# Expert loop of a hybrid decoder block: the narrow down product moves beside the wide one, into a PSUM bank of its own, and the wide gate turn moves ahead of the row turns

## The chip, the cores and the metric

The kernel runs on one NeuronCore of a Trainium2 chip. The metric is the device time in microseconds (us) of one execution. It is the median of three runs, and lower is better. The profile is of one further execution, and its own time stands beside its span in the table below.

## What is computed

One decoder layer on 512 tokens of width 1024 in float32: a mixer (gated linear attention, sparse attention, mLSTM) and then a mixture of 64 experts. The change is in the experts alone:

```python
w = sigmoid scores of the 6 chosen experts, normalised, times 2.5; gates[t, e] = w or 0
a = einsum('td,edf->tef', xb, w_gate);  u = einsum('td,edf->tef', xb, w_up)     # d = 1024, f = 256
routed = einsum('tef,efd->td', silu(a) * u * gates, w_down)
shared = (silu(t @ s_gate) * (t @ s_up)) @ s_down
return routed + shared
```

Only the rows that were routed to an expert are multiplied by its weights, so each chosen (token, expert) pair is one row of work, and the 3 MB of weights of an expert are read once for each unit of rows that uses them.

## The kernel before, in words

**Units and steps.** The routed rows are packed into units. A wide unit has up to 128 rows of one expert, a narrow unit up to 64 rows of one expert. One step of the expert loop works on one wide and one narrow unit. The number of steps is found at run time; here there are 31, of which 30 are iterations of a hardware loop that every engine runs (`with pe.Fori(0, more) as i` and its like on ACT, DVE, POOL and SP), and one stands behind the loop. The loop is software-pipelined: iteration i ends with the wide gate and up product of step i+1.

**Weights.** A step needs six pieces of 1 MB, each with one buffer in `ring`: of the wide expert piece 0 and 1 (gate and up columns, for two halves of d) and piece 2 (down), and the same three of the narrow expert. `load_piece(e, b, k)` issues them on SP's queue (L629 for gate and up, two DMAs each; L633 for down), b = 0 for wide, 1 for narrow. SP issues in program order, and waits ahead of each until the buffer is free: wide 0 and 1 (of step i+1), narrow 2 (of step i, free when `down_used` tells that the last narrow down product is done), wide 2 (of step i+1), narrow 0 and 1 (of step i+1).

**Wide products.** They are exact to nearly float32 by a split: ACT copies a wide piece to a rounded high part (`gate_hi` L1782, `down_hi` L1789), DVE subtracts to get the low part (`weights_lo`, L2477), which also frees the ring buffer. The same is done to the rows (`turned`, L1795 and L2497) and to the gated activations (`act_turned`, L1812 and L2532). PE makes high*high, low*high and high*low products: `gate_up` (L1351 and L1355, 24 matmuls into bank 2) and `down` (L1410, 12 matmuls into banks 4 and 5).

**Narrow products.** They are plain float32, straight from the ring: `gate_up_narrow` (L1368, into bank 3) and `down_narrow` (L1394, which went into bank 4, so that it had to wait until DVE had read the wide result out of that bank, `y_read`).

**Turns.** PE transposes: the gathered rows of the wide unit (`turn`, L1331, banks 0 and 1) and of the narrow unit (`turn_narrow`, L1338, bank 7, read by ACT's L1800), the gated activations of the wide unit (`act_turn`, L1377, bank 6) and of the narrow one (`act_turn_narrow`, L1383, bank 6, read by ACT's L1812).

**Between.** ACT's silu is L1806, DVE's product with it L2504 (`gated`). DVE scales the results out of PSUM into `ys` (`store_y` L2518, `store_narrow` L2526), and POOL scatters them to `y_dram` (L812) and gathers the rows of later units (L785) by indirect DMA. `store_narrow` waits until the narrow scatter of the step before has landed (`y_stored1`).

**Order.** Each engine's order is written out by hand, and engines meet only at semaphores. Behind the loop come `down` and `down_narrow` of the last step (the last narrow one went into bank 7 already), the load of the six result rows of each token, their sum, and the final norm.

Of the kernel before, what the change touches and what calls it, by code (L numbers as in the profile page):

```python
# [145 lines left out]
def hybrid_kernel(nc, a, out):  # L146
# [7 lines left out]
    WIDE, NARROW = 128, 64  # L154
# [8 lines left out]
    with ctx:  # L163
        sems = {}

        def sem(name):
            if name not in sems:
                sems[name] = ctx.enter_context(nc.semaphore(name))
            return sems[name]
# [11 lines left out]
        bank = [ctx.enter_context(nc.psum_tensor(f"bank{i}", [P, 512], F32)) for i in range(BANKS)]  # L181
# [148 lines left out]
        w_raw = [pieces(ringf, w_at[b]) for b in range(2)]  # L330
        w_shd = w_raw[0][0].rearrange("p (m n) -> p m n", m=2)
        diag = w_raw[0][1].rearrange("p (i k t) -> p i k t", i=TT, t=P)
        LAST_NARROW = 7
        SUMMED = (3, 3, 3, 2)
        w_hi, w_lo = pieces(arenap, 0), pieces(arenap, 6144)
        re.at = 12288
# [3 lines left out]
        ys = [rx.take(D) for _ in range(2)]  # L340
# [6 lines left out]
        ae = ro.take(2, NARROW)  # L347
# [496 lines left out]
        def _(pe):  # L844
            mm = nc.tensor.matmul
# [125 lines left out]
            for f in range(2):  # L971
                b = begin(f"kd{f}")
                for i in range(TT):
                    ins = nc.tensor.transpose(b[:, tile_cols(i)], kd[:, f, tile_cols(i)], ident[:, :])
# [10 lines left out]
            for l in range(8):  # L985
# [5 lines left out]
                for tp in range(2):  # L991

                    pair = [begin(f"scA{l}{2 * hh + tp}") for hh in range(2)]
                    for ii in range(2):
                        for f in range(2):
                            t = tile_cols(2 * tp + ii)
                            for hh, b in enumerate(pair):
                                r_ = slice(64 * hh, 64 * hh + 64)
                                ins = mm(b[:, tile_cols(2 * ii + f)], ksrc[r_, f, t], qsrc[r_, f, t], start=True, stop=True)
# [8 lines left out]
            for h in range(5):  # L1008
                if h < 4:
                    b = begin(f"oA{h}")  # L1010
                    for i in range(TT):
                        if i:
                            mm(b[:, tile_cols(i)], state[:, i - 1, h // 2, :], qcz[h % 2][:, h // 2, tile_cols(i)],
                               start=True, stop=False)
                        ins = mm(b[:, tile_cols(i)], va[:, i, tile_cols(h)], S[:, h % 2, i, h // 2, :],
                                 start=(i == 0), stop=True)
# [13 lines left out]
            for i in range(TT):  # L1030
                ins = nc.tensor.transpose(b[:, 4 * i:4 * i + 4], g4[3][:, tile_cols(i)], ident[0:4, 0:4])
# [14 lines left out]
            for h in range(4):  # L1046
# [11 lines left out]
                if h == 3:  # L1058
                    pe.wait_ge(sem("squares_ready"), 9)
                    b = begin("msq")  # L1060
                    for k in range(2):
                        ins = mm(b[:, :], ones[:, :], sqB[:, k, :], start=(k == 0), stop=(k == 1))
# [5 lines left out]
                for j in range(TT):  # L1068
                    pe.wait_ge(sem("SW_ready"), 4 * h + j + 1)
                    ins = mm(b[:, P * j:T], vc[:, j, tile_cols(h)], SW[:, j, P * j:T], start=(j == 0), stop=(j == 3))  # L1070
                end(ins)
                b = begin(f"den{h}")
                for j in range(TT):
                    ins = mm(b[:, P * j:T], ones[:, :], SW[:, j, P * j:T], start=(j == 0), stop=(j == 3))
# [24 lines left out]
            for i in range(TT):  # L1099
                ins = nc.tensor.transpose(b[:, 32 * i:32 * i + 32], small[0:32, tile_cols(i)], ident[0:32, 0:32])  # L1100
# [48 lines left out]
            for n in range(-1, 8):  # L1149
                if n < 7:  # L1150
                    i, g = divmod(n + 1, 2)
# [11 lines left out]
                i, g = divmod(n, 2)  # L1163
# [163 lines left out]
            def turn(half):  # L1327

                rows = xg[0].rearrange("t (p j) -> t j p", j=8)
                for q in range(4):  # L1330
                    ins = nc.tensor.transpose(bank[half][:, tile_cols(q)], rows[:, 4 * half + q, :], ident[:, :])  # L1331
                ins.then_inc(sem("turned"), 1)
# [39 lines left out]
            def act_turn(i):  # L1372

                pe.wait_ge(sem("acte_ready"), 2 * i + 1)
                rows = acte[0].rearrange("t (p m) -> t m p", m=2)
                for m in range(2):
                    ins = nc.tensor.transpose(bank[6][:, tile_cols(m)], rows[:, m, :], ident[:, :])  # L1377
                ins.then_inc(sem("acte_turned"), 1)

            def act_turn_narrow(i):  # L1380

                pe.wait_ge(sem("acte_ready"), 2 * i + 2)
                nc.tensor.transpose(bank[6][:, 0:P], acte[1][:, 0:P], ident[:, :]).then_inc(sem("acte_turned"), 1)  # L1383

            def down_narrow(i, out=4):

                w = w_raw[1][2].rearrange("p (m n) -> p m n", m=2)
                pe.wait_ge(sem("ae_hi_ready"), 2 * i + 2)
                pe.wait_ge(sem("w_loaded12"), 16 * i + 16)
                if out == 4:  # L1390
                    pe.wait_ge(sem("y_read"), 4 * i + 4)
                for m in range(2):
                    for n in range(2):
                        ins = mm(bank[out][NARROW * n:NARROW * n + NARROW, :], ae[:, m, :], w[:, m, 512 * n:512 * n + 512],  # L1394
                                 start=(m == 0), stop=(m == 1))
                ins.then_inc(sem("down_used"), 1)

            def down(i, turn_between=False):

                hi, lo = (w[2].rearrange("p (m n) -> p m n", m=2) for w in (w_hi, w_lo))  # L1400
                pe.wait_ge(sem("ae_hi_ready"), 2 * i + 1)
                pe.wait_ge(sem("ae_lo_ready"), i + 1)
                pe.wait_ge(sem("down_hi_ready"), i + 1)
                pe.wait_ge(sem("down_lo_ready"), i + 1)
                pe.wait_ge(sem("y_read"), 4 * i + 2)
                for n in range(2):
                    terms = [(t[:, m, :], w[:, m, 512 * n:512 * n + 512]) for m in range(2)
                             for t, w in ((ae_hi, hi), (ae_lo, hi), (ae_hi, lo))]
                    for q, (s_, w) in enumerate(terms):
                        ins = mm(bank[4 + n][:, :], s_, w, start=(q == 0), stop=(q == 5))  # L1410
                    ins.then_inc(sem("down_used" if n else "y_begun"), 1)
                    if turn_between and n == 0:
                        act_turn_narrow(i)
# [12 lines left out]
            with pe.Fori(0, more) as i:  # L1426

                gate_up_narrow(i)
                pe.wait_ge(sem("xg_loaded0"), 16 * i + 32)
                turn(0)  # L1430
                turn(1)
                down(i)
                act_turn_narrow(i)

                gate_up(i + 1)
                pe.wait_ge(sem("xg_loaded1"), 16 * i + 32)
                down_narrow(i)
                turn_narrow()
                act_turn(i + 1)
            gate_up_narrow(more)  # L1440
            down(more, turn_between=True)
            down_narrow(more, LAST_NARROW)

            def shared_down(i):
                for n in range(2):
# [27 lines left out]
        def _(act):  # L1473
# [317 lines left out]
            def turned(i):  # L1791

                for half in range(2):
                    act.wait_ge(sem("turned"), 3 * i + half + 1)
                    A(xe_hi[:, 512 * half:512 * half + 512], bank[half][:, :], ACT.Copy).then_inc(sem("xe_hi_ready"), 1)  # L1795
# [12 lines left out]
            def act_turned(i, b):  # L1808

                n = (FF, P)[b]  # L1810
                act.wait_ge(sem("acte_turned"), 2 * i + b + 1)
                A(ae if b else ae_hi, bank[6][:, 0:n].rearrange("p (m t) -> p m t", m=2), ACT.Copy  # L1812
                  ).then_inc(sem("ae_hi_ready"), 1)
# [8 lines left out]
            with act.Fori(0, more) as i:  # L1822

                act_turned(i, 0)
                gated(i, 1)
                turned(i + 1)
                for k in range(2):
                    gate_hi(i + 1, k, i)

                act_turned(i, 1)  # L1830
                gated(i + 1, 0)
                down_hi(i + 1, i)
                turned_narrow(i + 1)
# [14 lines left out]
        def _(dve):  # L1848
# [660 lines left out]
            def store_y(i, halves=(0, 1)):  # L2509

                dve.wait_ge(sem("y_stored0"), 16 * i + 16)
                for n in halves:
                    if n:
                        dve.wait_ge(sem("down_used"), 2 * i + 2)
                    else:
                        dve.wait_ge(sem("y_begun"), i + 1)
                    s_ = slice(512 * n, 512 * n + 512)
                    v.tensor_tensor(ys[0][:, s_], bank[4 + n][:, :], branch_gate[:, s_], ALU.mult).then_inc(sem("y_read"), 1)  # L2518

            def store_narrow(i, out=4):  # L2520

                dve.wait_ge(sem("y_stored1"), 16 * i + 16)
                dve.wait_ge(sem("down_used"), 2 * i + 3)
                for n in range(2):
                    s_ = slice(512 * n, 512 * n + 512)
                    v.tensor_tensor(ys[1][0:NARROW, s_], bank[out][NARROW * n:NARROW * n + NARROW, :], branch_gate[0:NARROW, s_],  # L2526
                                    ALU.mult).then_inc(sem("y_read"), 1)

            def act_turned(i):

                dve.wait_ge(sem("ae_hi_ready"), 2 * i + 1)
                v.tensor_tensor(ae_lo, bank[6][:, 0:FF].rearrange("p (m t) -> p m t", m=2), ae_hi.bitcast(F32),  # L2532
                                ALU.subtract).then_inc(sem("ae_lo_ready"), 1)
# [6 lines left out]
            with dve.Fori(0, more) as i:  # L2540

                act_turned(i)
                gated(i, 1)
                turned(i + 1)
                weights_lo(i + 1, 0)
                weights_lo(i + 1, 1)
                store_y(i)

                gated(i + 1, 0)
                store_narrow(i)  # L2550
                weights_lo(i + 1, 2)
            act_turned(more)
            gated(more, 1)
# [2 lines left out]
            v.tensor_tensor(w_shd, w_shd, branch_gate.rearrange("p (o n) -> p o n", o=1).to_broadcast([P, 2, D]), ALU.mult  # L2556
                            ).then_inc(sem("mr_ready"), 1)
            store_y(more, halves=(1,))
            store_narrow(more, LAST_NARROW)

            dve.wait_ge(sem("extra_loaded"), 128)
            def root_inverse(i):
# [67 lines left out]
```

## Time and profile before

| | us |
|---|---|
| three runs | 1358.45, 1363.02, 1363.63 |
| median | 1363.02 |
| the profiled execution | 1364.75 |
| its span | 1362.7 |
| expert loop in it, about | 740 to 1312 |

Busy shares of the span: PE 92%, weight loads on PE 63%, DVE 64%, ACT 39%, POOL 22%. A share is a mean over stages with different limits, so the table alone says nothing of the loop. The DMA row of the page's slices and the views of single stretches of the loop do. Engine names with a q (SPq, ACTq) are the sequencer of that engine; "us to landing" is the time from the issue of a DMA until the last part of it has arrived.

### The profile page before, as it was taken

The numbers are of one execution on the slowest core, as the hardware profiler recorded it, in microseconds if no ns is written. First come the engines' busy times: TensorE is split into PE (matmuls) and PEld (weight loads), VectorE is DVE, ScalarE is ACT, GpSimd is POOL, SyncE is SP. The second block draws the span as 40 slices with busy tenths as digits, with TensorE's granted clock in tenths as the row PEclk, the third lists the DMA queues.
The fourth block names the chain that finished last, engine by engine and source line by source line (L and its number), as shares of the span: only waits on it lengthen the run. The fifth ranks groups of instructions, "written<-read, shape, count | busy, mean of one in ns | idle before, by whom it ended". The sixth has DMA issues, their size and how long they took to land.

```text
span 1362.7 us, 19349 instructions
## 1 busy us (share of the span) xinstructions
PE 1247.1 (92%) x6452; PEld 864.1 (63%) x6452; DVE 870.6 (64%) x1251; ACT 530.6 (39%) x706; POOL 301.0 (22%) x325
## 2 busy tenths in 40 slices
PE   4899999999998989999998999999999999999986
PEld 1597788555644458888965666555665566666642
DVE  1659685669997727445667666566665666666656
ACT  3723431444334634222222444444444444444412
POOL 1200100012411000000002354433334333444521
PEclk9899999889999999999989999999999999999988
DMA  9325322003217242224126999999999999999967
GB/s 312 98 94 173 106 62 86 31 16 102 84 44 249 78 155 92 93 93 174 61 98 214 408 402 410 393 399 395 401 388 386 381 378 377 375 357 354 373 230 307
DMA packets 126632, 314.55 MB, mean 231 GB/s; under 512 B 20277, under 2 KB 57466, under 8 KB 122106
## 3 DMA queue, kind: packets, MB, share of 16 engines
q1 hardware_dynamic: 112250, 288.73, 57.7%
q0 software_dynamic: 14336, 25.20, 5.0%
q8 instruction: 30, 0.49, 0.2%
q14 instruction: 16, 0.13, 0.0%
HBM read 308.62 MB, written 30.41 MB: 249 GB/s over the span
## 4 chain that ended last, share of the span: by engine, by line
PE 49%; DMA 29%; DVE 12%; ACT 4%; issue 4%; SPq 2%; POOL 0%; DVEq 0%; ACTq 0%; POOLq 0%
DMA ring<-in_exp_w_up 25%; PE bank L928 16%; PE bank L933 8%; PE bank L1368 4%; DVE arena_parts L2477 3%; DMA ring<-in_w_in 2%; DVE arena L2203 2%; ACT arena_parts L1782 2%; PE bank L1355 2%; DMA arena<-in_ada_w 2%; DVE top L2202 2%; PE bank L875 1%; PE bank L1351 1%; PE bank L1457 1%; PE bank L1394 1%
## 5 line engine op out<-in xcount | busy, mean ns | idle before, releaser
L2477 DVE TENSOR_TENSOR arena_parts<-ring,arena_parts 128x2048 fp32r<-128x2048 f32 x93 | 212.3, 2287 | 50.9 <-ACT arena_parts L1782 48.8
L1368 PE MATMUL bank<-ring,oTA 128*64 128x256 f32 x992 | 120.1, 388 | 31.9 <-DMA ring<-in_exp_w_up 23.6
L928 PE MATMUL bank<-hT_parts,ring_parts 128*128 128x512 f32 x344 | 141.9, 412 | 4.7 <-ACT ring_parts L1502 2.9
L928 PE MATMUL bank<-x_parts,ring_parts 128*128 128x512 f32 x344 | 136.4, 396 | 0.0
L1782 ACT ACTIVATE arena_parts<-ring 128x2048 fp32r<-128x2048 f32 x62 | 118.3, 1918 | 30.5 <-DMA ring<-in_exp_w_up 30.5
L1806 ACT ACTIVATE oTB<-bank 128x256 f32<-128x256 f32 (+1 forms) x62 | 20.5, 331 | 253.0 <-PE bank L1368 136.6
L1368 PEld LDWEIGHTS bank<-ring,oTA 128*64 128x64 f32 x992 | 68.3, 138 | 75.6 <-DMA ring<-in_exp_w_up 40.0
L1502 ACT ACTIVATE ring_parts<-ring 128x2048 fp32r<-128x2048 f32 (+1 forms) x38 | 64.8, 1711 | 116.6 <-DMA ring<-in_w_in 75.1
L812 POOL DMA_INDIRECT y_dram<-arena,row_of x62 | 61.0, 984 | 221.1 <-DVE arena L2518 188.4
L1351 PE MATMUL bank<-arena_parts,oTA_parts 128*128 128x512 f32 x248 | 100.2, 404 | 3.2 <-DVE oTC_parts L2497 1.8
L1887 DVE TENSOR_TENSOR ring_parts<-ring,ring_parts 128x2048 fp32r<-128x2048 f32 (+1 forms) x34 | 68.0, 2006 | 50.6 <-ACT ring_parts L1502 50.1
L1351 PE MATMUL bank<-arena_parts,oTC_parts 128*128 128x512 f32 x248 | 97.0, 391 | 0.0
L1410 PE MATMUL bank<-arena_parts,oTB_parts 128*128 128x512 f32 x372 | 93.3, 399 | 0.0
L2504 DVE TENSOR_TENSOR oTB<-bank,oTB 128x256 f32<-128x256 f32 (+1 forms) x62 | 22.2, 358 | 101.7 <-ACT oTB L1806 101.7
L933 PE MATMUL bank<-hT_parts,ring_parts 128*128 128x512 f32 x344 | 85.0, 389 | 0.0
L785 POOL DMA_INDIRECT arena<-h_dram,tok_of x62 | 72.2, 1164 | 52.6 <-POOL tok_of L798 52.6
L928 PEld LDWEIGHTS bank<-hT_parts,ring_parts 128*128 128x128 f32 x344 | 66.2, 193 | 26.5 <-issue 6.7
L798 POOL COPY tok_of<-toks 128x1 int32 (+1 forms) x62 | 65.5, 1056 | 73.4 <-PE bank L1338 47.7
L1355 PE MATMUL bank<-arena_parts,oTA_parts 128*128 128x512 f32 x248 | 72.2, 412 | 6.0 <-DVE arena_parts L2477 1.6
L1410 PEld LDWEIGHTS bank<-arena_parts,oTB_parts 128*128 128x128 f32 x372 | 67.5, 188 | 13.5 <-issue 0.4
L928 PEld LDWEIGHTS bank<-x_parts,ring_parts 128*128 128x128 f32 x344 | 66.0, 192 | 15.9 <-issue 2.4
L933 PEld LDWEIGHTS bank<-hT_parts,ring_parts 128*128 128x128 f32 x344 | 64.6, 188 | 13.4
(448 smaller groups left out, 2344.4 us busy)
## 6 DMA issues: line engine op xcount, KB each, us to landing
ring<-in_exp_w_gate SPq DMA_DIRECT2D x124, 512.0 KB, 7.3
ring<-in_exp_w_up SPq DMA_DIRECT2D x124, 512.0 KB, 13.8
ring<-in_exp_w_down SPq DMA_DIRECT2D x62, 1024.0 KB, 13.7
ring<-in_w_in SPq DMA_DIRECT2D x25, 1024.0 KB, 5.4
ring<-in_ada_w SPq DMA_DIRECT2D x16, 1024.0 KB, 5.7
arena<-in_ada_w SPq DMA_DIRECT2D x4, 2048.0 KB, 16.7
arena<-y_dram SPq DMA_DIRECT2D x4, 1536.0 KB, 11.2
x<-in_x SPq DMA_DIRECT2D x2, 2048.0 KB, 13.2
```

The source lines that it names most:

```text
L785: g.indirect_dma_start(out=xg[b][0:n], out_offset=None, in_=h_dram[:, :], in_offset=bass.IndirectOffsetOnAxis(ap=rows[0:n] if rows is not ...
L798: g.tensor_copy(dst[:, :], lists[:, bass.ds(u, 1)]).then_inc(sem("list_copied"), 1)
L928: mm(out, w if weights_left else t, t if weights_left else w, start=(j == 0 and k == 0), stop=False)
L933: ins = mm(out, w if weights_left else t, t if weights_left else w, start=False, stop=(j == n - 1))
L1351: mm(out_gu, t[:, tile_cols(4 * k + j)], hi[:, :, j, :], start=(k == 0 and j == 0 and x_ == 0), stop=False)
L1355: ins = mm(out_gu, xe_hi[:, tile_cols(4 * k + j)], lo[:, :, j, :], start=False, stop=(k == 1 and j == 3))
L1368: ins = mm(bank[3][r_, 0:FF].rearrange("p (g f) -> p g f", g=2), xe[:, 4 * k + j, :], w[:, :, j, tile_cols(h)], start=(k == 0 and j == 0), ...
L1410: ins = mm(bank[4 + n][:, :], s_, w, start=(q == 0), stop=(q == 5))
L1502: A(hi_view(name, 1, n), ring_view(name, 0, 1, n), ACT.Copy).then_inc(sem("hi_split"), 1)
L1782: A(w_hi[k], w_raw[0][k], ACT.Copy).then_inc(sem("gu_hi_ready"), 1)
L1887: v.tensor_tensor(lo_view(name, 1, n), ring_view(name, 0, 1, n), hi_view(name, 1, n).bitcast(F32), ALU.subtract).then_inc(sem("lo_split"), 1)
L2477: v.tensor_tensor(w_lo[k], w_raw[0][k], w_hi[k].bitcast(F32), ALU.subtract).then_inc(sem("gu_lo_ready" if k < 2 else "down_lo_ready"), 1)
```

## The change

On PE the narrow turn of the activations moves ahead of `down(i)`, and `down_narrow(i)` directly behind it, in bank 7 instead of bank 4. Its wait on `y_read` goes. Bank 7 is also that of `turn_narrow`, so PE now waits until DVE has read the narrow result (`y_read` 4i+6) ahead of `act_turn(i+1)` and `turn_narrow`, and these two change places. On ACT the copy of the narrow turned activations moves ahead of the two `gate_hi` copies. On DVE `store_narrow(i)` moves ahead of `gated(i+1, 0)`. SP's and POOL's programs are not edited.

```diff
-            def down_narrow(i, out=4):
+            def down_narrow(i):
                 w = w_raw[1][2].rearrange("p (m n) -> p m n", m=2)
                 pe.wait_ge(sem("ae_hi_ready"), 2 * i + 2)
                 pe.wait_ge(sem("w_loaded12"), 16 * i + 16)
-                if out == 4:
-                    pe.wait_ge(sem("y_read"), 4 * i + 4)
                 for m in range(2):
                     for n in range(2):
-                        ins = mm(bank[out][NARROW * n:NARROW * n + NARROW, :], ae[:, m, :], w[:, m, 512 * n:512 * n + 512],
+                        ins = mm(bank[7][NARROW * n:NARROW * n + NARROW, :], ae[:, m, :], w[:, m, 512 * n:512 * n + 512],
                                  start=(m == 0), stop=(m == 1))
                 ins.then_inc(sem("down_used"), 1)
...
                 turn(0)
                 turn(1)
+                act_turn_narrow(i)
                 down(i)
-                act_turn_narrow(i)
+                down_narrow(i)
 
                 gate_up(i + 1)
                 pe.wait_ge(sem("xg_loaded1"), 16 * i + 32)
-                down_narrow(i)
+                pe.wait_ge(sem("y_read"), 4 * i + 6)
+                act_turn(i + 1)
                 turn_narrow()
-                act_turn(i + 1)
...
                 gated(i, 1)
                 turned(i + 1)
+                act_turned(i, 1)
                 for k in range(2):
                     gate_hi(i + 1, k, i)
 
-                act_turned(i, 1)
                 gated(i + 1, 0)
...
                 store_y(i)
+                store_narrow(i)
 
                 gated(i + 1, 0)
-                store_narrow(i)
                 weights_lo(i + 1, 2)
```

`store_narrow` reads `bank[7]` in the same way, and `LAST_NARROW` is gone.

## Rows read from the trace of the kernel before

**Rows 1.** The page's slices (40 of 34.1 us): DMA busy in tenths, and GB/s.
```profile
DMA  9325322003217242224126999999999999999967
GB/s 312 98 94 173 106 62 86 31 16 102 84 44 249 78 155 92 93 93 174 61 98 214 408 402 410 393 399 395 401 388 386 381 378 377 375 357 354 373 230 307
```

**Rows 2.** Busy by stretch of 60 us: engines, clock, DMA share, GB/s.
```profile
800.00:860.00 60.00, 55.82 (x329) 38.10 (x329) 39.15 (x40) 26.23 (x34) 28.09 (x28) 1.00 1.03 409
...
1160.00:1220.00 60.00, 57.17 (x322) 38.83 (x317) 38.00 (x40) 28.76 (x35) 28.64 (x30) 1.00 1.00 363
```

**Rows 3.** The chain that ended last, 940 to 1000 us: start, us, what.
```profile
954.90 16.37 DMA ring<-in_exp_w_up
```

**Rows 4.** The same chain, 760 to 800 us.
```profile
767.21 3.67 PE bank L1368 x32
...
776.83 1.20 PE bank L1355 x4
778.03 1.84 PE bank L1351 x8
779.87 0.91 PE bank L1355 x4
780.78 1.87 PE bank L1394 x8
782.64 1.04 PE bank L1338 x8
...
784.43 3.67 PE bank L1368 x32
```

**Rows 5.** Timeline, 950 to 970 us: start, us, what, [idle before <-releaser].
```profile
952.35 1.95 PE L1368 MATMUL bank<-ring,oTA 128*64 128x256 f32 x16 [0.84 <-DMA ring<-in_exp_w_up]
955.15 3.00 PE L1410 MATMUL bank<-arena_parts,oTB_parts 128*128 128x512 f32 x12
957.98 0.27 PE L1383 MATMUL bank<-ident,oTB 128*128 128x128 f32 x1
960.54 0.26 ACT L1812 ACTIVATE oTB<-bank 128x128 f32<-128x128 f32 x1
963.55 0.38 SPq L629 DMA_DIRECT2D ring<-in_exp_w_up  x1
964.24 0.38 ACT L1806 ACTIVATE oTB<-bank 128x256 f32<-128x256 f32 x1 [3.44 <-PE bank L1355]
964.66 0.42 DVE L2504 TENSOR_TENSOR oTB<-bank,oTB 128x256 f32<-128x256 f32 x1 [0.50 <-ACT oTB L1806]
966.33 3.84 SPq L633 DMA_DIRECT2D ring<-in_exp_w_down  x2
```

**Rows 6.** Three single issues, of 963, 966.3 and 1282.5 us: size, us to landing.
```profile
ring<-in_exp_w_up SPq DMA_DIRECT2D x1, 512.0 KB, 14.9
...
ring<-in_exp_w_down SPq DMA_DIRECT2D x1, 1024.0 KB, 15.4
...
ring<-in_exp_w_down SPq DMA_DIRECT2D x1, 1024.0 KB, 12.9
```

**Rows 7.** Line L1377 over the span: ns min/median/max, first and last start.
```profile
L1377 PE MATMUL bank<-ident,oTB x62: 281/334/388, 746.6 to 1301.5; 128*128 128x128 f32 x62
```

**Rows 8.** Waits of SP's queue, 760 to 1330 us: us in total, times, longest.
```profile
SPq L633 <- PE bank L1394: 59.0, 30, 10.0
```

**Rows 9.** Timeline of the last step and of one narrow scatter.
```profile
772.04 0.94 POOL L812 DMA_INDIRECT y_dram<-arena,row_of  x1 [0.91 <-POOL row_of L798]
...
1282.58 3.84 SPq L633 DMA_DIRECT2D ring<-in_exp_w_down  x2
...
1302.14 3.67 PE L1368 MATMUL bank<-ring,oTA 128*64 128x256 f32 x32 [0.33 <-ACT oTA L1800]
...
1308.92 2.29 DVE L2556 TENSOR_TENSOR ring<-ring,arena 128x2048 f32<-128x2048 f32 x1 [0.77 <-DMA ring<-in_sh_w_down]
...
1311.73 1.40 DVE L2526 TENSOR_TENSOR arena<-bank,arena 64x512 f32<-64x512 f32 x2
```

**Rows 10.** DMA issues by line, 760 to 1330 us: median us to landing.
```profile
y_dram<-arena,row_of POOLq DMA_INDIRECT x62, 7.3
```

More of the change, by code:

```diff
@@ L332, in hybrid_kernel @@
         diag = w_raw[0][1].rearrange("p (i k t) -> p i k t", i=TT, t=P)
-        LAST_NARROW = 7
         SUMMED = (3, 3, 3, 2)
@@ L1431, in _ @@
                 turn(1)
+                act_turn_narrow(i)
                 down(i)
-                act_turn_narrow(i)
+                down_narrow(i)
                 gate_up(i + 1)
                 pe.wait_ge(sem("xg_loaded1"), 16 * i + 32)
-                down_narrow(i)
+                pe.wait_ge(sem("y_read"), 4 * i + 6)
+                act_turn(i + 1)
                 turn_narrow()
-                act_turn(i + 1)
             gate_up_narrow(more)
             down(more, turn_between=True)
-            down_narrow(more, LAST_NARROW)
+            down_narrow(more)
             def shared_down(i):
@@ L2518, in store_y, with store_narrow @@
                     v.tensor_tensor(ys[0][:, s_], bank[4 + n][:, :], branch_gate[:, s_], ALU.mult).then_inc(sem("y_read"), 1)
-            def store_narrow(i, out=4):
+            def store_narrow(i):
                 dve.wait_ge(sem("y_stored1"), 16 * i + 16)
@@ L2525, in store_narrow @@
                     s_ = slice(512 * n, 512 * n + 512)
-                    v.tensor_tensor(ys[1][0:NARROW, s_], bank[out][NARROW * n:NARROW * n + NARROW, :], branch_gate[0:NARROW, s_],
+                    v.tensor_tensor(ys[1][0:NARROW, s_], bank[7][NARROW * n:NARROW * n + NARROW, :], branch_gate[0:NARROW, s_],
                                     ALU.mult).then_inc(sem("y_read"), 1)
@@ L2558, in _ @@
             store_y(more, halves=(1,))
-            store_narrow(more, LAST_NARROW)
+            store_narrow(more)
             dve.wait_ge(sem("extra_loaded"), 128)
```

## The prediction

> **What bounds the kernel now.** I read the page's slices first. The last third of the span is one loop, and in its slices the DMA engines are 90% busy or more and move 350 to 410 GB/s, where most slices ahead of it stand far lower [rows 1]. The table of 60 us stretches gives the shares of the same time: DMA 1.03 at 409 GB/s early and 1.00 at 363 GB/s late, with PE at 55.8 and 57.2 of 60 us and TensorE's granted clock at 1.00, its level of 2.4 GHz [rows 2]. So both PE and DMA look full, and the chain of waits must say which one ends last. Early in the loop, at 767 to 784 us, the chain runs through PE, with stretches of ACT and DVE in it, and one step takes 784.43 - 767.21 = 17.2 us [rows 4]. From some 830 us on it is another chain: a DMA of the narrow expert's second gate and up piece takes 16.4 us to land, and PE's `gate_up_narrow` waits for it [rows 3, 5]. The mean step is (1301.5 - 746.6) / 30 = 18.5 us, from the first and the last of the 31 wide gate turns [rows 7]. So for most of the loop PE could go 1.3 us faster in a step than the weights let it.
>
> The weights land in the order of their issue: the wide expert's piece 1 was issued at 963.55 and landed 14.9 us later, at 978.5; the narrow down piece was issued at 966.33 and landed 15.4 us later, at 981.7 [rows 5, 6]. The issues are 2.8 us apart and the landings 3.3 us. A DMA that lands 15 us after its issue while one lands every 3 us has four others ahead of it. I conclude that the DMA side works off a queue, and that the time of an issue matters little as long as the queue isn't empty. Six landings at 3.1 us are the 18.5 us step.
>
> **The change part by part.** The change adds no instruction and no byte. It moves PE's work, and with it two kinds of wait.
>
> (1) The wait of `down_narrow` for DVE's read of bank 4 goes. It was hidden: `down_narrow` came so late that the steps are set elsewhere. Worth 0 to 0.4 us in a step of the PE-bound kind, counted in (3).
>
> (2) `down_narrow` frees the narrow down buffer earlier. SP waited 59.0 us for it in 30 steps, 2.0 us each [rows 8]. The new free time is ahead of `gate_up`, and SP then only has its own order, behind wide piece 1, to respect: the issue comes up to 2.0 us earlier. The queue being FIFO, I take the landing as unchanged; the bound on the other side is a landing 2.0 us earlier.
>
> (3) PE's own cycle, if it waits for no DMA. Its parts in the new order, from the start of `gate_up_narrow`: that product 3.67 [rows 4]; row turns until `down` starts 955.15 - (952.35 + 1.95) = 0.85 [rows 5]; the narrow gate turn 0.27, whose silu and product run beside the row turns (even the wide ones, 0.38 and 0.42, fit in 0.85) [rows 5]; `down` 957.98 - 955.15 = 2.83 [rows 5]; `down_narrow` 1.87; `gate_up` 2 x (1.84 + 0.91) = 5.50 [rows 4]; then PE stands still until the wide silu and product are made, from 964.24 to 964.66 + 0.42 on ACT and DVE, 0.84 and a hand-over, 0.9 in all [rows 5]; the wide gate turn 0.3 [rows 7]; the narrow row turn 1.04; and ACT's copy of it until the next `gate_up_narrow`, 784.43 - (782.64 + 1.04) = 0.75 [rows 4]. The sum is 18.0 us, against 17.2 before. Two things changed in it: the stall of the low gate weights inside `gate_up` is covered now, since `gate_up` starts 1.87 us later, and the 0.9 us of silu and product, which `down_narrow` and the narrow row turn covered before, lies bare. The bounds of that 0.9: not below 0.84, as it is a true dependence; above, DVE may be inside one of its 128x2048 passes, 2.29 us, or inside the narrow store, 1.40 us [rows 9], when the silu is ready. I take 0.9, since both passes of that time end a microsecond or more earlier by rows 4, where the second low product (779.87) already stands behind them.
>
> (4) ACT's copy of the narrow turn, 0.26 us [rows 5], now stands ahead of the two high copies, and delays the low weights by 0.3. Hidden, because PE comes to them 1.9 us later than it did; without that cover it would be 0.3 x 30 = 9 us.
>
> (5) DVE's `store_narrow` stands ahead of `gated(i+1, 0)`, and waits for the narrow scatter of the step before. That was issued at 772.04, 1.2 us behind the end of `gate_up_narrow`, and such a scatter takes 7.3 us [rows 4, 9, 10]: it lands 8.5 us behind that end. The store wants to start at about 10. Cost 0, with 1.5 us in hand. Behind it on DVE stand `gated` and so PE's gate turn, then the low down weights and SP's next issue. POOL's `gather(1)` waits for the narrow row turn, which comes later by 0.9 less what the step gains; its rows are wanted a step later. Cost 0.
>
> (6) The new DMA wait. `down_narrow` wants its weights at the end of `down`, 0.85 + 0.27 + 2.83 = 3.95 us behind the end of `gate_up_narrow`. In the step above that end was 971.3 + 1.95 = 973.3, where 971.3 is the landing of rows 3, so they are wanted at 977.2 and land at 981.7. That is 4.5 us late. PE will wait there, once; the whole cycle then shifts against the DMA stream, and the waits for gate and up weights go, as these land ahead of the narrow down piece. From then on PE waits 18.5 - 18.0 = 0.5 us a step at `down_narrow`. The queue stays fed: the buffers are held longer by the shift of 4.5 us, and of 15 us of queue some 10 remain. So the loop keeps the DMA's pace, and the steps cost nothing.
>
> (7) The shift has to be paid once, at the end. The last narrow down piece of a loop iteration was issued at 1282.58 and landed 12.9 us later, at 1295.5 [rows 6, 9]. In the new order `down_narrow` starts there, and the last `gate_up_narrow` ends 1.87 + 5.50 + 0.9 + 0.3 + 1.04 + 0.75 + 3.67 = 14.0 us later, at 1309.5. It ended at 1302.14 + 3.67 = 1305.8 [rows 9]. That is 3.7 us later. Behind it DVE's product of the shared weights had waited 0.77 us for a DMA [rows 9], which it won't now: 2.9 us. If the landing is 2.0 us earlier, by (2), it is 0.9 us.
>
> The sum against the profiled execution's own 1364.75 is 1367.7. It is 1.7 us above the median of the runs, 1363.0; on that the same 2.9 us give **1366**.
>
> One rule of the Trainium skill speaks against a loop bound by DMA rate. "DMA: Bandwidth & Descriptors", section Bandwidth, measured 425 GB/s for long transfers and puts the fabric's ceiling at 435. The trace shows 409 at best and 363 late [rows 2]. By that page of the Trainium skill there would be headroom of 4 to 17%, and a step at 425 GB/s would take, as an estimate from that page, about 18 us or less, no longer than PE's new cycle. The same section says that the HBM side binds HBM loads at about 358, which the trace's 409 contradicts; the measurement decides.
>
> **The rivals.** *The loop is bound by time to landing and not by rate.* For it: the rate falls from 409 to 363 GB/s while the share stays at 1.00, so busy isn't the same as full speed. Against it: landings come in a steady rhythm whatever the gap of the issues. Then the earlier issue of (2) is a gain, and the loop goes at PE's 18.0 us: 30 x 0.5 = 15 us less, 1348 to 1352. (This is what the Trainium skill's "DMA: Bandwidth & Descriptors", section Bandwidth, would lead to.)
>
> *The bare gate decides.* If silu and product stand behind `store_narrow` on DVE, because its scatter lands later than the 1.5 us in hand or because the passes ahead of it end late, then PE's cycle is above 18.0. It decides from 18.5 on, which is 0.5 us more than I reckon. With 1.0 us more, 19.0 us, the loop takes 30 x 0.5 = 15 us more, and with the end's 3 us the time is 1381.
>
> *Nothing moves.* The narrow down piece lands as much earlier as it is issued, the shift is 2 us smaller, and the end hides the rest: 1363 to 1364.
>
> **How the numbers follow.** Forecast 0.52, with its own range 1360 to 1371; landing-bound and faster 0.11; bare gate and slower 0.21; nothing moves 0.16. What a measurement of this kernel can tell from no change is 0.5%, 6.8 us. Slower by more than that takes the bare gate and 0.05 of the forecast, where the shift or the cycle is a little larger: 0.26. Faster takes the first rival: 0.11. The rest, 0.63, is within. The range 1357 to 1378 leaves out most of the faster case and the worse half of the slower one.
>
> **What would show it.** In the profile after: SP's wait of 59 us for L1394 gone; PE waiting at the narrow down product for `in_exp_w_down`, some 15 us in total, and no longer at L1368 for `in_exp_w_up`; the chain through `in_exp_w_down`; DMA share still 1.00 at the same GB/s; the first steps at 18.0 and not 17.2 us; a wait of the gate turn for DVE's L2504 of 0.9 us a step; the loop's end some 3 us later. It is wrong if the steps in the middle are longer than 18.8 us with DMA share below 1 (bare gate), or shorter than 18.2 us with a higher rate.

## The result, and the profile after

The changed kernel takes 1415.83 us (median of 4 runs, 1410.16 to 1416.94) against 1360.74 us for the kernel before (4 runs, 1356.21 to 1363.63). The ratio is 1.038, with a 95% interval of 1.0349 to 1.041: 3.8% slower. The forecast was 1366, its range ended at 1378. The profiled execution took 1415.85 us, 51.1 us more than the 1364.75 of before. One run of e8_fill_both below, of 1820.34 us, was in a slow state of the chip (granted clock 0.652) and is left out of its figures.

In the text PE is TensorE, ACT is ScalarE, DVE is VectorE, POOL is GpSimd and SP is the engine that issues the weight loads. A "slow product" is a `gate_up_narrow` whose matmuls, with no wait among them, take 5.06 us and more instead of 3.67.

The page's slices of the changed kernel, with TensorE's granted clock in tenths ahead of the two rows that answer to [rows 1]:

```profile
PEclk9999999899999999999999999999999999999988
DMA  8325222003227053341339999999999999999947
GB/s 304 95 88 178 90 89 83 1 15 120 89 90 238 1 202 100 99 148 56 135 127 394 363 359 359 378 369 363 380 362 369 353 355 325 331 336 327 340 178 310
```

The DMA engines are 90% busy and more, as before, but the rate is 8 to 51 GB/s lower in each full slice of the loop. The clock row says nothing: its digit is 9 for anything between 0.90 and 1. The 60 us stretches, which answer to [rows 2], tell more (engines busy, then clock, DMA share, GB/s):

```profile
800.00:860.00 60.00, 54.63 (x283) 37.22 (x281) 33.84 (x37) 23.58 (x31) 19.34 (x24) 0.91 0.99 367
...
860.00:920.00 60.00, 54.63 (x293) 36.74 (x289) 35.84 (x37) 25.56 (x31) 19.37 (x24) 0.94 0.99 369
...
1160.00:1220.00 60.00, 54.63 (x282) 36.75 (x282) 34.82 (x36) 23.59 (x31) 18.51 (x23) 0.91 0.96 336
```

The mean granted clock was 1.00 here and is 0.91 to 0.94. And the chain of waits over one step of the changed kernel, 949 to 971 us, answers to [rows 4] (start, us, what; the lines have moved by one to three: gate_up_narrow is L1367, down L1407, down_narrow L1391, gate_up L1350 and L1354):

```profile
949.79 5.36 PE bank L1367 x32
955.15 1.09 PE bank L1330 x8
956.23 0.11 PE bank L1382
956.34 2.90 PE bank L1407 x12
959.24 1.87 PE bank L1391 x8
961.11 2.07 PE bank L1350 x8
963.18 0.92 PE bank L1354 x4
964.10 1.81 PE bank L1350 x8
965.91 0.92 PE bank L1354 x4
966.83 0.02 issue
966.85 0.39 ACT oTB L1804
967.25 0.02 issue
967.27 0.44 DVE oTB L2502
967.71 0.14 issue
967.84 0.48 PE bank L1376 x2
968.32 1.04 PE bank L1337 x8
969.36 0.02 issue
969.38 0.61 ACT oTA L1798
969.99 0.12 issue
970.11 2.15 PE bank L1367 x9
```

There are three things to see. No DMA stands in this chain, where the chain of before went through one for 16 of 19 us [rows 3]. The silu, the product and ACT's copy lie bare, as the prediction said. And the same 32 matmuls of `gate_up_narrow` that took 3.67 us take 5.36. In this step the granted clock falls from its level of 2.4 GHz to that of 1.2 GHz (0.50 in the rows) just behind the start of that product and comes back while it still runs (half-microsecond stretches, same columns as above):

```profile
949.00:949.50 0.50, 0.02 (x1) 0.00 (x0) 0.50 (x1) 0.44 (x1) 0.30 (x1) 1.00 0.75 205
949.50:950.00 0.50, 0.21 (x2) 0.22 (x4) 0.50 (x1) 0.43 (x2) 0.50 (x1) 0.90 0.96 295
950.00:950.50 0.50, 0.50 (x4) 0.27 (x3) 0.50 (x1) 0.00 (x0) 0.50 (x1) 0.50 0.88 295
...
952.50:953.00 0.50, 0.50 (x6) 0.32 (x4) 0.00 (x0) 0.00 (x0) 0.50 (x2) 0.50 1.05 426
953.00:953.50 0.50, 0.50 (x6) 0.26 (x4) 0.00 (x0) 0.00 (x0) 0.11 (x1) 0.68 1.07 426
953.50:954.00 0.50, 0.50 (x8) 0.37 (x6) 0.00 (x0) 0.00 (x0) 0.00 (x0) 1.00 1.21 459
```

Three of the 30 steps don't have that, those whose `gate_up_narrow` starts at 890.88, 1071.70 and 1252.59 us. Here is the first, from the chain of 870 to 900 us:

```profile
870.55 5.36 PE bank L1367 x32
...
886.68 0.92 PE bank L1354 x4
...
890.88 3.67 PE bank L1367 x32
```

That `gate_up_narrow` follows 20.33 us behind the one ahead of it, which was slow. The step that it begins itself is 18.63 us long, as the next one starts at 909.51. Between `gate_up`'s end (966.83) and `gate_up_narrow` (970.11) PE does ten transposes in 3.28 us and otherwise stands still, for 1.0 and for 0.75 us. Then come 1.69 us of loss at 1.2 GHz. The kernel before has in that place 1.87 us of matmuls of `down_narrow`, the ten transposes and 0.4 us of standing still.

The mean step, from the wide gate turn as in [rows 7]:

```profile
L1376 PE MATMUL bank<-ident,oTB x62: 281/320/385, 746.7 to 1350.2; 128*128 128x128 f32 x62
```

It is (1350.2 - 746.7) / 30 = 20.12 us, against 18.50. Thirty times the difference is 48.6 of the 51.1 us. A mean of 20.12 where a step without a slow product takes 18.63 means some 45 us for the 27 slow products (seven of them take 5.06 to 5.30 us and not 5.36).

### The profile page after: what moved, and what is told of

Same layout as the page of the kernel before. It is cut to its first block, busy times and chain, and to the rows that moved or that the text cites. A ratio compares the mean times of both kernels' runs of the same rounds, so it can differ in the third digit from the quotient of the medians.

```text
span 1413.7 us, 19349 instructions
## 1 busy us (share of the span) xinstructions
PE 1282.9 (91%) x6452; PEld 893.4 (63%) x6452; DVE 865.2 (61%) x1251; ACT 525.8 (37%) x706; POOL 266.3 (19%) x325
## 4 chain that ended last, share of the span: by engine, by line
PE 79%; DVE 10%; ACT 4%; DMA 3%; issue 3%; SPq 0%; POOL 0%; DVEq 0%; ACTq 0%; POOLq 0%
PE bank L927 16%; PE bank L1367 11%; PE bank L1350 9%; PE bank L932 8%; PE bank L1407 6%; PE bank L1354 4%; PE bank L1391 4%; PE bank L1330 2%; PE bank L1337 2%; DVE arena L2201 2%; DMA arena<-in_ada_w 1%; DVE top L2200 1%; PE bank L874 1%; ACT oTA L1798 1%; PE bank L1455 1%
## 5 line engine op out<-in xcount | busy, mean ns | idle before, releaser
L1367 PE MATMUL bank<-ring,oTA 128*64 128x256 f32 x992 | 160.0, 494 | 24.3 <-ACT oTA L1798 24.3
L1367 PEld LDWEIGHTS bank<-ring,oTA 128*64 128x64 f32 x992 | 92.7, 179 | 81.9 <-issue 65.9
L1350 PE MATMUL bank<-arena_parts,oTA_parts 128*128 128x512 f32 x248 | 100.6, 406 | 1.8 <-DVE oTC_parts L2495 1.8
L1350 PE MATMUL bank<-arena_parts,oTC_parts 128*128 128x512 f32 x248 | 97.3, 392 | 0.0
L1407 PE MATMUL bank<-arena_parts,oTB_parts 128*128 128x512 f32 x372 | 93.5, 400 | 0.0
L1407 PEld LDWEIGHTS bank<-arena_parts,oTB_parts 128*128 128x128 f32 x372 | 67.3, 188 | 17.1 <-issue 0.5
L784 POOL DMA_INDIRECT arena<-h_dram,tok_of x62 | 62.4, 1006 | 52.6 <-POOL tok_of L797 52.6
L1350 PEld LDWEIGHTS bank<-arena_parts,oTA_parts 128*128 128x128 f32 x248 | 46.5, 187 | 35.7 <-issue 26.3
```

The source lines that it names most:

```text
L784: g.indirect_dma_start(out=xg[b][0:n], out_offset=None, in_=h_dram[:, :], in_offset=bass.IndirectOffsetOnAxis(ap=rows[0:n] if rows is not ...
L1350: mm(out_gu, t[:, tile_cols(4 * k + j)], hi[:, :, j, :], start=(k == 0 and j == 0 and x_ == 0), stop=False)
L1367: ins = mm(bank[3][r_, 0:FF].rearrange("p (g f) -> p g f", g=2), xe[:, 4 * k + j, :], w[:, :, j, tile_cols(h)], start=(k == 0 and j == 0), ...
```

## The experiments

Times are medians; each ratio is to runs of the kernel before on the same chip. "Mean step" is always read from the row of the wide gate turn, as above. e5 and e6 leave out half of each narrow expert's down weights, so what they compute isn't the layer; the others compute what the kernel before computes.

### Is it the clock, or only the longer chain?

```diff
                 pe.wait_ge(sem("xg_loaded1"), 16 * i + 32)
+                for _ in range(4):                                     # e1_fill, e8_fill_both
+                    mm(bank[3][:, 0:P], ident[:, :], causal[:, :], start=True, stop=True)
                 pe.wait_ge(sem("y_read"), 4 * i + 6)
                 act_turn(i + 1)
                 turn_narrow()
+                for _ in range(3):                                     # e8_fill_both alone
+                    mm(bank[3][:, 0:P], ident[:, :], causal[:, :], start=True, stop=True)
```

> The changed kernel with four float32 128x128 matmuls into bank 3, whose results nobody reads, placed behind gate_up(i+1), where PE stands still for the silu and product of the wide gate. The output is unchanged. Theory (clock): after the change PE does only transposes and waits for 3.3 us of each step, its granted clock falls to 1.2 GHz for 3.4 us, and gate_up_narrow takes 5.36 instead of 3.67 us in most steps; that is 44 us of the 52. Then the filler brings the clock back to 1.00, gate_up_narrow to 3.67 us, steps to 18.6 to 19.0 us, and the time to 1366 to 1380 us. Rival (chain): the bare silu and product lengthen the chain and the clock is beside the point: 1415 us or a little more, with gate_up_narrow at 5.4. Rival (DMA): the lower DMA rate of 360 GB/s is the cause: 1415 us, unchanged.

Measured: 1396.34 us, ratio 1.0224 (1.0161 to 1.0287). Work that nobody reads makes the kernel some 19 us faster. Stretches of 60 us in e1_fill:

```profile
860.00:920.00 60.00, 57.31 (x307) 39.82 (x305) 33.85 (x36) 24.54 (x30) 19.36 (x24) 0.91 0.96 358
920.00:980.00 60.00, 57.30 (x328) 41.45 (x327) 38.88 (x41) 24.54 (x30) 19.41 (x24) 1.00 1.01 388
```

With the same work PE does 307 matmuls in one stretch and 328 in the next, and what differs is the clock. The size was wrong, 1366 to 1380 expected: the filler took away about half of the slow products, not all. The second gap was still open.

> The kernel of e1_fill with three more such matmuls behind the narrow row turn, where PE stands still for ACT's copy (0.75 us). Output unchanged. Theory (clock): e1_fill took the clock drop out of half the steps (18.63 against 20.33 us); with the second gap filled too it goes from nearly all, the steps are 18.6 to 18.9 us throughout, and the time is 1366 to 1376 us. Rival (chain): the filler is only more work; 1396 us or more.

Measured: 1377.13 us (median of three, 1374.64 to 1379.88), ratio 1.0103 (1.003 to 1.0177), a little above the 1366 to 1376 expected. In its trace:

```profile
800.00:860.00 60.00, 59.60 (x349) 43.52 (x348) 37.41 (x42) 24.98 (x32) 20.44 (x25) 1.00 1.02 396
...
932.66 13.12 DMA ring<-in_exp_w_down
...
956.82 3.60 PE bank L1367 x32
...
L1376 PE MATMUL bank<-ident,oTB x62: 283/320/388, 748.9 to 1313.3; 128*128 128x128 f32 x62
```

The clock is 1.00, `gate_up_narrow` takes 3.60 us, the mean step is 18.81 us. With both gaps filled and the dependences of the change as they were, some 38 of the 55 us are gone. So the clock is the larger part of the loss. Most of the rest is the step: 18.81 against 18.50 us, 9.4 us in 30. In this trace the loop also starts 2.3 us later than in that of before (748.9 against 746.6) and what lies behind it is 0.5 us longer. The DMA that PE now waits for is that of the narrow down weights, which is step (6) of the prediction, visible only once the clock is back.

### Which part of the change opens the gap?

> The kernel before with one edit: act_turn(i+1) ahead of turn_narrow(), and down_narrow(i) still between gate_up and the two. Theory (clock): the silu and product stay covered by down_narrow (1.9 us), so that there is no new idle time and no clock drop: 1358 to 1366 us, the same. Rival (chain, the place of the wide gate turn as such): the narrow rows are turned 0.3 us later, steps of the PE-bound kind grow by 0.3, at most 1370 us.

```diff
                 down_narrow(i)
-                turn_narrow()
                 act_turn(i + 1)
+                turn_narrow()
```

Measured: 1361.28 us, ratio 0.998 (0.9956 to 1.0005). The wide gate turn ahead of the narrow row turn costs nothing while `down_narrow` lies between it and `gate_up`.

> The kernel before with one part of the change: down_narrow stays behind gate_up but writes bank 7, so that the narrow row turn waits for DVE's store_narrow (and one unread 128x128 transpose into bank 3 takes that wait). Chain alone: PE stands still 1.4 us more, steps of 18.7 to 18.9 us, 1366 to 1372 us. Theory (clock): that is 1.4 + 0.75 us of standing still with transposes between, much as in the changed kernel, so the clock drops in many steps: 1385 to 1420 us.

```diff
-            def down_narrow(i, out=4):
+            def down_narrow(i, out=7):             # store_narrow the same
...
                 down_narrow(i)
+                pe.wait_ge(sem("y_read"), 4 * i + 6)
+                nc.tensor.transpose(bank[3][:, 0:P], ident[:, :], ident[:, :])
                 turn_narrow()
```

Measured: 1423.54 us, ratio 1.0468 (1.04 to 1.0535), so at least as slow as the whole change, and just above the 1385 to 1420 expected. Its waits and its mean step:

```profile
PE bank L1439 <- DVE arena L2528: 45.3, 30, 1.5
...
L1377 PE MATMUL bank<-ident,oTB x62: 281/385/492, 742.3 to 1354.5; 128*128 128x128 f32 x62
```

The wait for the narrow store is 1.5 us a step, and the step grows by 1.9, to 20.41: from another cause than in the changed kernel, PE stands still ahead of the transposes and again behind them, `gate_up_narrow` takes 5.1 us, and the clock is 0.91 in each stretch from 800 to 1280 us. Its first two steps, without a slow product, take 19.1 us, so even with the clock aside it would be above the 18.50. A bank of its own for the narrow product is only free of charge if nobody else needs that bank soon.

> The changed kernel with the narrow row turn ahead of the wide gate turn again (and the one unread 128x128 transpose that takes the wait), but with ACT's order as in the change: silu, down_hi (1.9 us), then the copy of the narrow rows. Theory (ACT's queue): gate_up_narrow waits for silu 0.4, down_hi 1.9, copy 0.75, together 3.1 us behind gate_up, hardly less than the 3.3 us of the changed kernel; the steps stay at 18.4 or 20.1 us and the clock still drops: 1395 to 1415 us. Rival (the order of the two turns on PE is the cause): 1360 to 1375 us as in e3_swap_act.

```diff
                 pe.wait_ge(sem("y_read"), 4 * i + 6)
+                nc.tensor.transpose(bank[3][:, 0:P], ident[:, :], ident[:, :])
+                turn_narrow()
                 act_turn(i + 1)
-                turn_narrow()
```

Measured: 1390.96 us, ratio 1.0205 (1.0149 to 1.026), below the 1395 to 1415 expected. The order of the two turns isn't the cause either. ACT's queue is what stands ahead of `gate_up_narrow` now (chain of e2_swap, 958 to 963 us):

```profile
958.63 0.92 PE bank L1354 x4
...
959.86 0.89 ACT arena_parts L1788
...
961.66 0.60 ACT oTA L1799
962.26 0.12 issue
962.38 3.67 PE bank L1367 x32
```

L1788 is `down_hi`, 1.9 us of which the last 0.9 are on the chain. In the kernel before, `down_narrow` covered it. The step without a slow product is 18.2 us, with one 19.9, and 20 of its 30 steps have one.

> The changed kernel with the narrow row turn ahead of the wide gate turn again, and ACT's copy of it (turned_narrow) ahead of down_hi, so that neither the silu nor the high down copy stands ahead of gate_up_narrow; one 128x128 transpose into bank 3 that nobody reads takes the wait for the narrow store. Theory (clock) and rival (chain) both: PE's gap behind gate_up shrinks from 3.3 us to about 2 us with transposes in it, the clock stays at 1.00, the engines' cycle is 17.2 to 17.6 us, and the loop is bound by its DMAs as before: 1358 to 1370 us. Rival (DMA, the early down_narrow makes the transfers worse): above 1390 us.

```diff
                 gated(i + 1, 0)
-                down_hi(i + 1, i)
                 turned_narrow(i + 1)
+                down_hi(i + 1, i)          # on top of e2_swap
```

Measured: 1373.83 us, ratio 1.0089 (1.0058 to 1.0121), outside what I expected, on the slow side. The engines' own cycle is short now, 17.4 us in the shortest steps, and another wait decides (of e3_swap_act, 760 to 1330 us):

```profile
PE bank L1391 <- DMA ring<-in_exp_w_down: 31.9, 19, 4.0
```

This is step (6) again. The prediction had 4.5 us once, and from then on, in each step, the difference between the DMAs' 18.5 us and PE's cycle; with a cycle of 17.4 that is 1.1 us, 33 us in 30 steps, and 31.9 are measured. But they don't come evenly: PE stands still 19 times, for up to 4.0 us. Behind six of the seven waits of over 2 us the clock falls, and it is 0.97 in five of the eight 60 us stretches from 800 to 1280 us.

> The kernel of e3_swap_act, with SP issuing the narrow down piece ahead of the wide pieces 0 and 1 of the next step, not behind them. In e3 PE waited up to 4.4 us at down_narrow for that piece (my step 6), and the steps with such a wait took 21 us because the clock dropped after it. If the order of issue is what makes that piece late, it lands two pieces (6 us) earlier in the queue, the waits at L1391 go from 73 us (weight loads, whole loop) to under 15, the clock stays at 1.00, and the loop goes at the pace of its DMAs: 1356 to 1366 us, the same as the kernel before or a little better. If the piece is late because the DMAs lag as a whole, another wait takes its place, with clock drops as in e3: 1368 to 1378 us.

```diff
+                en = expert(1, i)          # on top of e3_swap_act
+                sp.wait_ge(sem("down_used"), 2 * i + 1)
+                load_piece(en, 1, 2)
                 for k in range(2):
                     sp.wait_ge(sem("gu_lo_ready"), 2 * i + k + 1)
                     load_piece(e, 0, k)
-                en = expert(1, i)
-                sp.wait_ge(sem("down_used"), 2 * i + 1)
-                load_piece(en, 1, 2)
```

Measured: 1371.4 us, ratio 1.0058 (1.003 to 1.0086). The wait at `down_narrow` is gone altogether, and another has taken its place, the second of my two cases (e9_sp_order, 760 to 1330 us):

```profile
ACT arena_parts L1781 <- DMA ring<-in_exp_w_up: 44.4, 40, 2.8
```

> The kernel of e9_sp_order with three unread float32 128x128 matmuls into bank 3 between the wide gate turn and gate_up_narrow, where PE stands still for ACT's copy. Output unchanged. Theory (clock): if e9 still shows clock drops they go, and the time is 1356 to 1364 us; if e9 has none, 0.2 us a step at most is lost: within 0.3% of e9.

```diff
                 act_turn(i + 1)
+                for _ in range(3):                 # on top of e9_sp_order
+                    mm(bank[3][:, 0:P], ident[:, :], causal[:, :], start=True, stop=True)
```

Measured: 1370.27 us, ratio 1.0079 (1.005 to 1.0108), within the 0.3% of e9 and not the 1356 to 1364 of a kernel without clock drops. The drops that are left stand behind another stop (e10_sp_order_fill, 760 to 1330 us):

```profile
PE bank L1436 <- DVE arena L2527: 14.9, 13, 1.3
```

That is PE's wait for the narrow store, ahead of the row turns, and 8 of the 13 are followed by a drop within 2.5 us. The chain leads back from it over DVE to ACT's wait for `in_exp_w_up`. A filler behind the turns doesn't fill that stop. Neither kernel beats the one before.

> The changed kernel with ACT's order of before: the copy of the narrow turned activations behind the two high copies. down_narrow then waits for it: it is ready 6.1 us behind the end of gate_up_narrow and not 2.2, where down ends at 4.1 us. Chain alone: 2.0 us more a step, 20.6 us without a drop and 22.3 with one, 1430 to 1475 us; PE then stands still at a second place too, so the clock drops at least as often as in the changed kernel. If the place of that copy doesn't matter (something else covers it): 1416 us.

```diff
                 turned(i + 1)
-                act_turned(i, 1)
                 for k in range(2):
                     gate_hi(i + 1, k, i)
 
+                act_turned(i, 1)
```

Measured: 1437.9 us, ratio 1.0557 (1.0524 to 1.059), mean step 21.06 us by its row. The place of ACT's copy matters, and by the chain's sum. But I expected drops at least as often, and they are rarer, with a slow product in 11 of 30 steps (in five of these it takes 6.6 us); two stretches of e11_act_back:

```profile
800.00:860.00 60.00, 49.97 (x272) 33.56 (x270) 31.58 (x32) 24.54 (x30) 22.85 (x24) 0.94 0.97 366
...
1100.00:1160.00 60.00, 50.41 (x285) 35.06 (x285) 34.94 (x36) 24.12 (x29) 25.84 (x24) 1.00 0.95 346
```

PE is busy for 50 us of 60 and the clock is 0.94 to 1.00; in the changed kernel it is busy for 54.6 and the clock is 0.91.

### Are the two kernels bound by their DMAs?

```diff
-                    sp.dma_start(w_raw[b][2].rearrange("p (m n) -> p m n", m=2), src).then_inc(sem(f"w_loaded{b}2"), 16)
+                    h_ = 512 if b else 1024
+                    sp.dma_start(w_raw[b][2].rearrange("p (m n) -> p m n", m=2)[:, :, 0:h_], src[:, :, 0:h_]).then_inc(sem(f"w_loaded{b}2"), 16)
```

> The kernel before, but of each narrow expert's down weights only half the columns are loaded (0.5 instead of 1 MB; the products of the other half use what lay in the buffer). If the loop before is bound by its DMAs (my reading), 1/12 of the bytes less bring the mean step from 18.4 us to the PE-bound 17.2 us: 1322 to 1340 us. If it is bound by PE and waits between engines: 1356 to 1364 us.

Measured: 1334.48 us, ratio 0.98 (0.9759 to 0.9841).

> The changed kernel with half of each narrow expert's down weights loaded, as in e5_before_half (the products of the other half use what lay in the buffer). Theory (clock and chain): the changed kernel waits for no DMA, so fewer bytes bring nothing: 1410 to 1417 us, steps of 20.3 us. Rival (DMA): it gains as the kernel before did, 27 us: 1389 us.

Measured: 1409.8 us, ratio 1.0342 (1.0286 to 1.0398). The mean steps, e5_before_half first:

```profile
L1378 PE MATMUL bank<-ident,oTB x62: 281/334/388, 746.6 to 1271.4; 128*128 128x128 f32 x62
```

```profile
L1377 PE MATMUL bank<-ident,oTB x62: 281/320/385, 742.8 to 1344.4; 128*128 128x128 f32 x62
```

The kernel before falls from 18.50 to 17.49 us a step, close to the 17.2 of PE's own cycle, and the changed kernel stays at 20.05 of 20.12. So the kernel before is bound by its DMAs, as I had read it, and the changed one is not. The times to landing agree: a piece of `in_exp_w_up` lands 14.1 us after its issue in the kernel before and 7.7 us in the changed one (medians).

## Why the prediction was wrong

The forecast failed at step (3), in the sentence "PE stands still until the wide silu and product are made ... 0.9 in all". The 0.9 us were right as time: the chain shows 0.39 + 0.44 + 0.14 and two hand-overs, 1.0 us. What I left out is what that does to the clock of the work behind it. I took all PE terms from rows at 2.4 GHz and never asked if the new order keeps that level. The price of that is up to 1.69 us in each of 27 of 30 steps, some 45 us; e8_fill_both, whose clock stays at 1.00 in the loop, runs some 38 us faster than the changed kernel. The step that was to stay at 18.5 us takes 20.12.

Term by term, with the clock aside:

- (1), the wait on bank 4: hidden, as said. What took its place, the wait for the narrow store ahead of the turns, is hidden too in the changed kernel. e7_before_bank7 shows that it wasn't harmless in itself, and I had priced the move only in the order of the change.
- (2), SP's wait for `down_narrow`: 59.0 us before, 4.1 us after. Right, and worth nothing.
- (3), PE's own cycle: 18.0 us reckoned, 18.63 measured. The row turns with the gate turn took 1.20 and not 1.12, `down` 2.89 and not 2.83, `gate_up` 5.72 and not 5.50 (its first eight matmuls take 2.07 us when they directly follow the narrow ones), the bare silu and product 1.0 and not 0.9, the wide gate turn 0.48 and not 0.3 (the 0.3 is one transpose, and [rows 7] count 62 in 31 steps, so two a step). Even without the clock, 18.63 is above the 18.50 of the DMAs, so the bound passes from the DMAs to PE, which I had put 0.5 us on the other side.
- (4), (5): the low weights come in time and the narrow store too; no wait of DVE for a scatter stands in the changed kernel's waits.
- (6), (7): in the changed kernel they don't happen, because PE has become too slow to wait for a DMA. The wait of (6) is real in e3_swap_act and e8_fill_both, and in e3_swap_act its total is what (6) gives for a cycle of 17.4 us. I had treated 18.5 us as an even pace, while the steps of the kernel before vary from 17.2 to 19.7 us; so some waits are long, and what those do to the clock I hadn't priced here either.

Of the rivals, "the bare gate decides" had the right place and sign, with 0.21: it said that it decides from a cycle of 18.5 us on, and the cycle was 18.63. Its sign came too, steps longer than 18.8 us. But it priced 19.0 us at 1381, from late passes on DVE, and knew of no clock either. Against "bound by time to landing" speak e5_before_half, which gains 2% for 1/12 of the bytes of weights, and e9_sp_order, where an earlier issue only moved the wait. But the reading of 15 us to landing as four others ahead in one queue was too simple: of the 16 parts of the piece issued at 1282.58 us, 15 had landed 8.4 us later, and only the last took the 12.9 us of [rows 6].

The rule that I weighed, of headroom up to 425 GB/s (the Trainium skill, "DMA: Bandwidth & Descriptors", section Bandwidth), finds no support: no run here goes above 409 GB/s over a 60 us stretch from 800 us on. The rule that did matter was one I had left out. The Trainium skill, "TensorE: Matmul & The Clock Gate", section "A second HAM failure mode: psum-queue depth-cycling", tells of a kernel in which frequent short stops between groups of matmuls make the clock swing between its two levels. The traces agree: in the changed kernel's loop the clock is 0.91 to 0.94 with no stop of PE longer than about 1 us.

What stays open: why the drop comes in this place and not in another, and why three steps have none. In the changed kernel the fall creeps against the start of `gate_up_narrow`, mostly by some 0.15 us a step, from some 0.6 us ahead of it to 0.95 us behind it; then one step has none, and it begins anew. What PE does there is ten transposes with two short stops, 3.28 us in all; the kernel before has 0.4 us of stops around the same transposes and keeps 1.00, and e11_act_back has more standing still in all and fewer drops. Fillers show that work in the stops prevents it. Whether transposes count as work for the clock was not separated from the stops.

## What to carry to other kernels

When a change takes covering matmuls out of a stretch of transposes and short waits, price the work behind it at both levels of the clock. Ask of each filler product what it covers on all engines: `down_narrow` covered DVE's product, ACT's `down_hi` and the copy, and kept the clock up as well. If the loop is bound by its DMAs, a move of PE's work has little to gain and PE's slack to lose, here 1.3 us a step; none of the orders tried here was faster than the one before.

## What the runs showed of the hardware that I had not expected

- Four unread float32 matmuls of 128x128 a step, in a wait of 1.0 us, made a kernel 19 us faster, and seven made it some 38 us faster.
- The DMA share doesn't tell whether a loop is bound by its DMAs: it is 0.99 at 367 GB/s in the changed kernel, whose loop has no wait for one, and 1.00 at 363 GB/s late in the kernel before, where ACT waits for one four times and PE once in 60 us.
- PE's busy share doesn't tell the clock: 54.6 of 60 us at 0.91, 50.4 of 60 us at 1.00.
